# Two blocks on one core: x loaded in column halves between halves of the first weights, with products of zeros at the start

## The reference

```python
h = x @ w_in                                  # 1024 -> 2304 columns
qa, ka, va, qb, kb, vb = jnp.split(h, [...], axis=-1)
qa = rope(qa.reshape(bsz, t, A_Q_HEADS, HEAD_DIM), pos)
ka = rope(ka.reshape(bsz, t, A_KV_HEADS, HEAD_DIM), pos)
oa = windowed_gqa_sink(qa, ka, va, sink)
ob = neighborhood_attention(qb..., kb..., vb..., rpb)
return jnp.concatenate([oa, ob], axis=-1) @ w_out
```

## Time and profile before

| | us |
|---|---|
| median of 3 runs | 1730.23 |
| lowest and highest | 1729.38, 1731.04 |
| span of the profiled execution | 1727.7 |
| PE busy in it | 1700.7 (98%) |
| DVE, ACT, POOL busy | 1175.8, 922.0, 297.4 |

### The profile page before, as it was taken

How to read it: one execution, slowest core, us unless ns; L and a number is a source line. 1 busy time by engine, 2 the same in 40 slices (tenths; PEclk the granted TensorE clock), 3 DMA queues, 4 the chain that set the end, 5 groups by cost and what they waited for, 6 DMA issues and landing times.

```text
span 1727.7 us, 25216 instructions
## 1 busy us (share of the span) xinstructions
PE 1700.7 (98%) x9721; PEld 1458.1 (84%) x9721; DVE 1175.8 (68%) x1565; ACT 922.0 (53%) x1269; POOL 297.4 (17%) x162
## 2 busy tenths in 40 slices
PE   8999999999999999999999999999999999999999
PEld 8768888899888788878888978888888889878887
DVE  5887666778476875577666876666666667856665
ACT  4664444546674544465446566444554456664443
POOL 6003000675250130010000830000000006500000
PEclk9999999999999999999999999999999999999999
DMA  9425655556405575536564523665465554435652
GB/s 283 151 86 187 226 194 177 168 154 198 142 1 168 168 237 193 179 127 209 193 194 146 196 98 123 218 192 187 156 209 184 191 187 160 141 98 195 194 194 98
DMA packets 204268, 293.83 MB, mean 170 GB/s; under 512 B 6474, under 2 KB 169776, under 8 KB 204192
## 3 DMA queue, kind: packets, MB, share of 16 engines
q1 hardware_dynamic: 201072, 285.56, 50.6%
q0 software_dynamic: 2688, 6.47, 1.4%
q10 hardware_dynamic: 432, 0.75, 0.1%
HBM read 291.71 MB, written 1.05 MB: 169 GB/s over the span
## 4 chain that ended last, share of the span: by engine, by line
PE 89%; DVE 5%; ACT 4%; issue 1%; POOL 1%; DMA 0%; SPq 0%; ACTq 0%; DVEq 0%; POOLq 0%
PE acc L2078 30%; PE pg L2078 14%; PE pg L2152 13%; PE pg L2156 12%; PE pg L2155 6%; PE pg L2153 6%; PE acc L2616 1%; ACT w_hi L852 1%; PE pg L2603 1%; PE pg L2718 1%; ACT arena L1054 1%; PE pg L2198 1%; POOL w_lo L752 1%; ACT op L867 1%; DVE op L1421 1%
## 5 line engine op out<-in xcount | busy, mean ns | idle before, releaser
L1383 DVE TENSOR_TENSOR w_lo<-w_raw,w_hi 128x2048 fp32r<-128x2048 f32 x231 | 539.7, 2338 | 162.7 <-ACT w_hi L852 162.6
L852 ACT CAST w_hi<-w_raw 128x2048 fp32r<-128x2048 f32 x269 | 513.0, 1908 | 66.4 <-PE pg L2078 28.3
L2078 PE MATMUL acc<-w_hi,op 128*128 128x512 f32 x1600 | 517.5, 393 | 1.7 <-DVE op L2008 1.6
L2152 PE MATMUL pg<-op,w_hi 128*128 128x512 f32 x960 | 382.3, 398 | 7.0 <-DVE op L1413 1.9
L2156 PE MATMUL pg<-op,w_hi 128*128 128x512 f32 x960 | 379.7, 395 | 0.0
L2078 PEld LDWEIGHTS acc<-w_hi,op 128*128 128x128 f32 x1600 | 300.3, 188 | 66.9 <-issue 7.4
L2078 PE MATMUL acc<-w_lo,op 128*128 128x512 f32 x800 | 311.5, 389 | 0.0
L752 POOL TENSOR_TENSOR w_lo<-w_raw,w_hi 128x2048 fp32r<-128x2048 f32 x38 | 175.1, 4615 | 682.6 <-DVE w_lo L1383 630.2
L2155 PE MATMUL pg<-op,w_lo 128*128 128x256 f32 x960 | 267.6, 279 | 0.0
L2153 PE MATMUL pg<-op,w_lo 128*128 128x256 f32 x960 | 266.4, 277 | 0.0
L2078 PE MATMUL pg<-op,w_hi 128*128 128x256 f32 x1184 | 222.9, 287 | 2.9 <-DVE op L1421 1.2
(11 more groups left out here) (342 smaller groups left out, 1704.3 us busy)
## 6 DMA issues: line engine op xcount, KB each, us to landing
w_raw<-in_mlp_w SPq DMA_DIRECT2D x64, 1024.0 KB, 5.3
w_raw<-in_ffn_w_gate SPq DMA_DIRECT2D x44, 1024.0 KB, 5.3
w_raw<-in_ffn_w_up SPq DMA_DIRECT2D x44, 1024.0 KB, 5.3
w_raw<-in_ffn_w_down SPq DMA_DIRECT2D x44, 1024.0 KB, 4.8
w_raw<-in_ssm_w_in SPq DMA_DIRECT2D x24, 1024.0 KB, 5.3
w_raw<-in_w_in SPq DMA_DIRECT2D x20, 1024.0 KB, 5.1
w_raw<-in_attn_w_in SPq DMA_DIRECT2D x8, 1024.0 KB, 10.1
w_raw<-in_ssm_w_out SPq DMA_DIRECT2D x8, 1024.0 KB, 4.9
```

What stands on the lines that cost most here:

```text
L852: act.copy(w_hi[:, u % RING, :], w_raw[:, u % RING, :]).then_inc(hi_ready, 1)
L1383: dve.tensor_tensor(w_lo[:, s, :], w_raw[:, s, :], w_hi[:, s, :].bitcast(F32), ALU.subtract) \
L2078: ins = pe.matmul(psum, l, r, start=first and i == 0, stop=last and i == 2)
L2152: pe.matmul(bank, hi, joined, start=k == 0, stop=False)
```

## The change

SP loads x in four quarters: the first 512 columns of both token tiles behind the first half of unit 0, the other 512 columns behind its second half. Unit 1 is loaded in two halves of rows as well, and cast, split and multiplied by halves like unit 0; its second column group gets a bank of acc, so that its copy out of PSUM (L1092) becomes two. The rope constants are loaded behind unit 2 instead of ahead of it, and have a semaphore of their own, rope_in.

ACT and DVE do banks 0 and 1 of x behind their part of the first half of unit 0, and banks 2 and 3 behind that of the second half. PE starts with 11 products of zeros once DVE has written the zeros, transposes the first half of x, does 7 more products of zeros, then the first 12 products of unit 0, and only then transposes the second half of x.

```diff
@@ SP
+            def load_x(a):
+                for t in range(TT):
+                    sp.dma_start(X[:, t, a * 512:(a + 1) * 512], A["x"][0, t * P:(t + 1) * P, a * 512:(a + 1) * 512]) \
+                        .then_inc(x_in[2 * a + t], 16)
+
+            sp.dma_start(half_unit(w_raw, 0, 0), v_att[:, 0:KC // 2, 0:U]).then_inc(first_raw[0], 16)
+            load_x(0)
+            sp.dma_start(half_unit(w_raw, 0, 1), v_att[:, KC // 2:KC, 0:U]).then_inc(raw_ready[0], 16)
+            load_x(1)
+            sp.dma_start(half_unit(w_raw, 1, 0), v_att[:, 0:KC // 2, U:2 * U]).then_inc(first_raw[1], 16)
+            sp.dma_start(half_unit(w_raw, 1, 1), v_att[:, KC // 2:KC, U:2 * U]).then_inc(raw_ready[1], 16)
+            for n in range(2, A_UNITS):
                 load(U_ATT + n, columns(v_att, n * U) if n < 7 else half_rows(v_att, 7 * U, n - 7))
-                if n == 1:
+                if n == 2:
-                    sp.dma_start(att_c[:, 0:n_rope], A["consts"][:, P:P + n_rope]).then_inc(const_in, 16)
+                    sp.dma_start(att_c[:, 0:n_rope], A["consts"][:, P:P + n_rope]).then_inc(rope_in, 16)
@@ ACT
-            turn("x", None, None)
-            act.wait_ge(raw_ready[0], 16)
-            act.copy(w_hi[:, 0, UN // 2:UN], w_raw[:, 0, UN // 2:UN]).then_inc(hi_ready, 1)
-            split(1)
+            for u in range(2):
+                act.wait_ge(first_raw[u], 16)
+                act.copy(half_unit(w_hi, u, 0), half_unit(w_raw, u, 0)).then_inc(first_hi, 1)
+                if u == 0:
+                    turn_banks("x", None, None, 0, 2)
+                act.wait_ge(raw_ready[u], 16)
+                act.copy(half_unit(w_hi, u, 1), half_unit(w_raw, u, 1)).then_inc(hi_ready, 1)
+                if u == 0:
+                    turn_banks("x", None, None, 2, 4)
...
-                    act.copy(q_raw[:, 1, :], bank).then_inc(attn_evac, 1)
+                    act.copy(q_raw[:, 1, 0:T], bank[:, 0:T])
+                    act.copy(q_raw[:, 1, T:2 * T], acc[:, 2, 0:T]).then_inc(attn_evac, 1)
@@ DVE: the same order as ACT, with the splits into w_lo
@@ PE
-            turn("x", X)
+            def turn_x(a):
+
+                for t in range(TT):
+                    pe.wait_ge(x_in[2 * a + t], 16)
+                    for j in range(4 * a, 4 * a + 4):
+                        ins = turn_chunk(X, j, t)
+                        if t == 1 and j % 2 == 1:
+                            ins.then_inc(turned, 1)
+
+            pe.wait_ge(fixed_ready, 1)
+            warm(acc[:, 0, :], 11)
+            pe.wait_ge(ident_in, 16)
+            turn_x(0)
+            warm(acc[:, 0, :], 7)
...
-                elif n == 0:
-                    pe.wait_ge(first_lo, 1)
+                elif n < 2:
+                    pe.wait_ge(first_lo, n + 1)
                     for k0, c in ((0, 0), (0, 1), (4, 0), (4, 1)):
+                        if n == 0 and c and not k0:
+                            turn_x(1)
                         if k0 and not c:
                             take(u)
                         for k in range(k0, k0 + 4):
-                            if c == 0 and k % 2 == 0:
+                            if n == 0 and c == 0 and k % 2 == 0:
                                 pe.wait_ge(xt_ready, TURN_BANK["x"] + k // 2 + 1)
...
-                        pe.wait_ge(const_in, CONST_ROPE)
+                        pe.wait_ge(rope_in, 16)
```

More of the change, by code:

```diff
@@ L179 @@
 N_SUMS = 4 + 3 * DEPTH
-CONST_ROPE, CONST_ATT, CONST_SSM, CONST_BLK = 16, 32, 48, 64
+CONST_ATT, CONST_SSM, CONST_BLK = 16, 32, 48
 NA_ROWS = 6
@@ L432, in low_half, with half_unit @@
             return pg[:, b:b + 2, T:2 * T]
+        def half_unit(buf, u, a):
+            return buf[:, u, a * UN // 2:(a + 1) * UN // 2].rearrange("p (k n) -> p k n", k=KC // 2)
         rel_dram = nc.dram_tensor("rel_scratch", (DH, 384), F32, kind="Internal").ap()
@@ L440, in two_blocks @@
         unit_done = sem("unit_done")
-        x_in = [sem(f"x_in{t}") for t in range(TT)]
-        first_raw = sem("first_raw")
+        x_in = [sem(f"x_in{q}") for q in range(2 * TT)]
+        first_raw = [sem(f"first_raw{u}") for u in range(2)]
         first_hi = sem("first_hi")
@@ L445, in two_blocks @@
         par_in = sem("par_in")
+        rope_in = sem("rope_in")
         const_in = sem("const_in")
@@ L1585, in _ @@
             dve.memset(sink[:, AQ:16], NEG).then_inc(fixed_ready, 1)
[L1586 to L1593, removed]
+            for u in range(2):
+                dve.wait_ge(first_hi, u + 1)
+                dve.tensor_tensor(half_unit(w_lo, u, 0), half_unit(w_raw, u, 0), half_unit(w_hi, u, 0).bitcast(F32),
+                                  ALU.subtract).then_inc(first_lo, 1)
+                if u == 0:
+                    turn_banks("x", None, 0, 2)
+                dve.wait_ge(hi_ready, u + 1)
+                dve.tensor_tensor(half_unit(w_lo, u, 1), half_unit(w_raw, u, 1), half_unit(w_hi, u, 1).bitcast(F32),
+                                  ALU.subtract).then_inc(lo_ready, 1)
+                if u == 0:
+                    turn_banks("x", None, 2, 4)
             def rope_sum(dst, plain, turned_ps, width):
@@ L1652, in _ @@
                     if n == 1:
-                        dve.wait_ge(const_in, CONST_ROPE)
+                        dve.wait_ge(rope_in, 16)
                     dve.wait_ge(rot_done, i + 1)
@@ L2218, in turn @@
                 ready = NORM_AT[name]
-                if name == "x":
-                    pe.wait_ge(ident_in, 16)
                 for t in range(TT):
-                    if name == "x":
-                        pe.wait_ge(x_in[t], 16)
                     for j in range(KC):
@@ L2447, in _ @@
                         for k in range(k0, k0 + 4):
-                            if c == 0 and k % 2 == 0:
+                            if n == 0 and c == 0 and k % 2 == 0:
                                 pe.wait_ge(xt_ready, TURN_BANK["x"] + k // 2 + 1)
                             o = k * U + c * P
-                            ins = three(acc[:, 3, 0:T] if c else bank[:, 0:T], wslice(u, o, o + P),
+                            ins = three(acc[:, 3 - n, 0:T] if c else bank[:, 0:T], wslice(u, o, o + P),
                                         (op_hi[:, k, :], op_lo[:, k, :]), k == 0, k == KC - 1)
```

9 lines of the change are left out of this document (removed).

## The result

The changed kernel takes 1735.94 us, the median of 7 executions (1731.44 to 1736.33); the kernel before takes 1729.83, also of 7 (1729.38 to 1731.04). The ratio is 1.0032 [1.0022, 1.0041]: 6.1 us slower, where 1730.0 and no change had been forecast. The profiled execution took 1736.19 with a span of 1734.2, 6.5 more than the span of before. Of the 7 executions one took 1731.44, and six lie between 1735.45 and 1736.33. This gap is a second fact to explain, and the profiled execution is one of the six.

A forecast was written before the change was run, and what follows sets the result against it. PE was taken to bound the kernel, busy for 98% of the span, with DVE close second. A saving of 0.33 us against 0.14 for x's rows gave -0.2 on 1730.23: 1730.0 us, 8 in 10 within 1727.9 to 1731.2.

The forecast's parts named there:

- The zeros from 1.0 us: Start of PE: 11 products of zeros from about 1.0 to 5.6 us, free because nothing else could run.
- near 9: Start of unit 0 on PE: the first product near 9 us, where it was at 10.35 before.
- unit 1 at 15.9: End of unit 0 on PE: at 15.9 us instead of 17.11, so unit 1 begins about 1.2 us sooner.
- the scheme: At unit 3: PE ready at 31.2, but DVE's split ends at 31.43, so 1.2 us of saving become 0.99.
- PE's saving: Unit 0 on PE: about 1.2 us sooner, bounds 0.1 lost and 2.4 gained; 0.33 left after the scores.
- DVE's split of unit 3: Before unit 3's products: split taking 2.32 us, ending at 31.43, moved only by the 0.14 us delay from x's rows.
- Somewhat less of it: DVE's splits: a sooner DVE might meet more of GpSimd's bias sums; one meeting made a split 3.18 instead of 2.29.
- rival (a): Unit 3's weights: issued sooner than 13.35, land sooner, PE's whole saving of 1.2 us counts, 1729.0 to 1727.8; chance 0.17.
- b and more: Unit 3's cast after 27.7: x's rows cost 0.41 us or more against a saving of 0.33, 1730.3; rival's chance 0.18.
- priced at 0.14, at most 0.41: Loads of x: rows of 2 KB instead of 4 KB delay unit 3 and the end by 0.14 us, bounds 0 and 0.41.
- rival (c): PE's stop before x: clock falls back to 1.2 GHz for all of unit 0, PE 5.2 us late, 1735.4; chance 0.03.
- PE wants it only at the end of unit 2: Unit 1's evacuation: two ACT copies add 0.16 us, hidden by the wait for unit 4's weights.

The follow-up runs named there:

- x whole: Changed kernel with x loaded as two whole tiles where its first halves stood: 1731.0 us, ratio 1.0014; six executions at 1729.92 to 1731.07, four at 1734.34 to 1735.44.
- Quarters alone: Kernel before with x loaded as four quarters in its old place, nothing else: 1732.87 us, ratio 1.0015.
- Zeros alone: Kernel before with 13 products of zeros on PE ahead of its first transposes, nothing else: 1729.84 us, ratio 1.0005.
- the sums on DVE: GpSimd's eight bias sums moved to DVE, behind its split of unit 2: 1728.87 us in the kernel before, 1729.31 in the changed kernel.
- Kept up: Changed kernel with 28 more products of zeros on PE ahead of unit 3: 1734.72 us, ratio 1.0029.
- changed, no zeros: Changed kernel without its 18 products of zeros: 1730.33 us, ratio 1.0005.
- only the first eleven zeros: Changed kernel without the seven products of zeros between the first transposes and the first product: 1735.68 us, ratio 1.0033.

## Why the prediction was wrong

**What was right.** The zeros from 1.0 us (1.04); the first product "near 9" (8.96), all products of unit 0 at 0.12 from there; unit 1 at 15.9 (15.79); and the scheme, that at unit 3 DVE's split comes close behind PE (by 0.99 in the prediction, 1.55 by the chain). PE's saving was as sized, and what it would meet at unit 3 was the right question.

**The step that failed: DVE's split of unit 3.** The prediction let it end at 31.43 and shift by 0.14. It took as given that the split takes 2.3 us when it is requested, and counted collisions with GpSimd only as "Somewhat less of it" in rival (a), one meeting of 0.89 us (3.18 less 2.29). It ended at 36.97, 5.54 later: 1.39 by the cast, 4.15 by the hold. Before, PE's chain came to unit 3 at 32.98, 1.55 after the split was done; after, 0.06 after it. So 5.54 less 1.55, plus 0.06, is the 4.05 of the two chains above. The rows to see it by were there: the sums, 24.63 to 38.9, stand across the splits of units 3 and 4, and a sum of 1.2 us that averages 1.79 (14.29 / 8) says that GpSimd had been waiting for DVE. I read from this who loses, GpSimd, and not that it could be the other way round.

The Trainium skill has the rule, and I had not weighed it: "SBUF — State Buffer", Who interferes with whom, says that a DVE instruction with two SBUF inputs contends with a GpSimd instruction that reads SBUF, that the shared port pair is an exclusive lock, and that the order of issue decides who is blocked. The trace agrees as far as one instruction goes: a split of 3.17 is 2.29 and the rest of a sum. If the lock changed hands after each instruction, though, a split would wait for the rest of one sum, at most 1.2 us, as in the profiled execution with x whole, whose split took 3.31 and which took 1730.93; the 6.47 us show DVE blocked through the rest of sum 5 and the three after it, without getting in between them.

**The landing, mis-sized.** The prediction's own sign for this was a cast after 27.7 ("b and more"); it came at 28.56. Rival (a), a sooner landing by a sooner issue, did not come in: SP issued unit 3 at 11.06 instead of 13.35, and it took 17.48 us instead of 13.8. The quarters were priced at 0.14, at most 0.41, from the bytes and the length of rows. Quarters alone cost 0.8, the whole change 1.39. The price was built on the rate of queued transfers whose share of the engines is full; after, the share itself was 0.90 to 0.95, and the rate 263 to 292 GB/s. With quarters alone the rate was 336 to 363 over the same two microseconds. Zeros alone also brought unit 3 late, by 0.8 (27.25 to 28.02 with the sums on DVE) to 1.4.

**The clock** was rival (c), but in the wrong place. It was to fall in the gap before x, and in the profiled execution it did not: the wait was 0.65 us. In the changed kernel with x whole it did, with a wait of 1.26 us (granted 0.54 from 9 to 12 us). In the changed kernel itself it fell in a wait of 4.8 us that no rival had. That (c)'s 1735.4 is close to what came out is chance. Kept up, it would have left 1734.7 or less.

**A cover that was thinner than said.** The two copies of unit 1's evacuation were to be hidden, because "PE wants it only at the end of unit 2". They stand behind the cast of unit 3; that was now 1.4 later, and unit 2's end sooner, so PE waited for them:

```profile
31.07 1.13 PE L2488 MATMUL acc<-arena 128*128 128x512 f32 x2 [0.32 <-ACT arena L1105]
```

It cost nothing, because PE then waited for DVE in any case.

**Where the 1.2 us went without the hold.** PE's saving was real, but unit 3 can't be split before its weights are there, and they came later by about as much (28.75 in the changed kernel with the sums on DVE, 27.25 in the kernel before). Brought forward by 2 us, they were no longer last, and the scores came 1.2 sooner. That part of the forecast, "no change", stands once both kernels have the sums on DVE: 1729.31 against 1728.87.

**The chances.** Slower by over 0.2% had 0.03. All my rivals were priced by one engine's shift or one transfer's; none was a change in which of two engines waits for the other.

**What stays open.** What decides whether DVE gets in between two of GpSimd's sums or not. Profiles show the hold in six executions, one of each of six kernels; that the other long ones, and not the short ones, were held is read from their times alone, the 1731.44 of the changed kernel included. The shares of long executions were 4 of 127 (before), 1 of 10 (zeros alone), 1 of 10 (changed, no zeros), 4 of 10 (changed, x whole), 5 of 10 (quarters alone), 6 of 7 (changed), 6 of 6 (only the first eleven zeros). The point within a sum does not decide it alone. Also open: why products of zeros make unit 3 land later at nearly the same rate of transfer (309 against 311 GB/s over 12 to 28 us).

## What to carry to other kernels

Before a gain on the bounding engine is credited, find what comes second at the next meeting point and ask with whom that engine shares a resource; a wait that the other engine takes today can be yours after a shift of a microsecond. When two engines shut each other out, place the flexible work where its own engine is idle anyway (here 4.91 us in a wait of 8 us), rather than tune the meeting. Look at all execution times, not at the median alone: a few long ones in the kernel before were most likely the same trouble, seen early.

## What was not expected of the hardware

- A DVE instruction of 2.3 us with both inputs in SBUF was kept out by GpSimd instructions end to end, 1.17 to 1.20 us each, through several of them (6.02 to 7.32 us in six kernels), while in other executions of the same kernel it must, by their times, have got in (five of ten with quarters alone).
- From 5 to 7 us, while x came in, 336 to 363 GB/s flowed with x in four transfers of 256 KB (rows of 2 KB) in its old place, and 263 to 292 with them between halves of units, against 393 to 418 with two of 512 KB. With the quarters alone, unit 1 landed 0.5 us later and unit 3's cast came 0.8 later.
- PE idle for 4.8 us: granted clock 0.56 at the end of it, 0.70 over the next 8.15 us, so partly the 1.2 GHz level of the two; 48 products took 8.16 us instead of 5.75.
- The clock column says 1.00 for the first products before and after alike, but they ran at 0.21 us each before and 0.12 after 18 products of zeros. The pitch shows the level there, the column doesn't.
